# Value products of an attention stage in 64-column halves, gathered by head into two output banks

## The reference

```python
# a: 6 heads of 64; each query sees its keys through three dilated windows, with a bias by distance
# b: 4 heads; p = softmax(s1) - lam * softmax(s2), v has 64 columns, then an rms norm over each head
# c: 6 heads; queries and keys of 64 + 32 columns from low-rank latents, v has 64 columns
attn = concat([a, b, c])        # 512 x 1024
x = layer_norm(alpha * x + attn @ w_o)
x = layer_norm(alpha * x + (silu(x @ w_gate) * (x @ w_up)) @ w_down)
```

## Time and profile before

| | |
|---|---|
| three runs | 1841.17, 1842.97, 1843.08 us |
| the profiled execution | 1841.61 us, span 1839.8 us |
| TensorE busy | 1803.4 us, 98% |
| TensorE weight loads | 1616.9 us, 88% |
| VectorE busy | 1219.3 us, 66% |
| ScalarE busy | 915.2 us, 50% |
| POOL busy | 776.9 us, 42% |
| HBM | 178.10 MB read, 100 GB/s over the span |
| second pair's attention, first layer | 747.3 to 831.1 us |
| second pair's attention, second layer | 1351.1 to 1435.0 us |

### The profile page before, as it was taken

How to read it: one execution, slowest core, us unless ns; L and a number is a source line. 1 busy time by engine, 2 the same in 40 slices (tenths; PEclk the granted TensorE clock), 3 DMA queues, 4 the chain that set the end, 5 groups by cost and what they waited for, 6 DMA issues and landing times.

```text
span 1839.8 us, 32454 instructions
## 1 busy us (share of the span) xinstructions
PE 1803.4 (98%) x12438; PEld 1616.9 (88%) x12438; DVE 1219.3 (66%) x2469; ACT 915.2 (50%) x1789; POOL 776.9 (42%) x601
## 2 busy tenths in 40 slices
PE   9999999999999999999999999999999999999997
PEld 7898888878898888888999998888888899999886
DVE  5797475379364363885999984266379589998533
ACT  4242276474366465873545443327487355454323
POOL 2533262255553354344443335544424344433652
PEclk9999999999999999999999999999999999999999
DMA  8444141123221232102232323222320223323321
GB/s 334 172 172 168 16 115 59 69 74 135 102 48 55 88 133 104 58 2 92 93 109 99 115 92 136 89 88 99 108 87 2 92 70 116 106 102 115 115 92 46
DMA packets 37029, 182.33 MB, mean 99 GB/s; under 512 B 8289, under 2 KB 9185, under 8 KB 18957
## 3 DMA queue, kind: packets, MB, share of 16 engines
q1 hardware_dynamic: 30664, 168.89, 26.6%
q10 hardware_dynamic: 6212, 11.36, 2.0%
HBM read 178.10 MB, written 5.41 MB: 100 GB/s over the span
## 4 chain that ended last, share of the span: by engine, by line
PE 86%; DVE 7%; ACT 4%; issue 2%; POOL 1%; DMA 1%; DVEq 0%; SPq 0%; ACTq 0%
PE ps L1665 17%; PE ps L1667 17%; PE ps L1666 17%; PE ps L2379 7%; PE ps L2381 7%; PE ps L2380 7%; PE ps L2285 3%; PE ps L1745 2%; PE ps L1759 2%; PE ps L2199 2%; PE ps L2303 2%; PE ps L1726 1%; POOL w_lo L874 1%; ACT pt L1131 1%; ACT w_hi L1004 1%
## 5 line engine op out<-in xcount | busy, mean ns | idle before, releaser
L874 POOL TENSOR_TENSOR w_lo<-raw,w_hi 128x512 fp32r<-128x512 f32 (+1 forms) x343 | 477.0, 1423 | 624.2 <-ACT w_hi L1004 624.0
L1004 ACT ACTIVATE w_hi<-raw 128x1024 fp32r<-128x1024 f32 (+3 forms) x174 | 170.9, 1025 | 226.0 <-PE ps L1667 209.1
L980 POOL TENSOR_TENSOR w_lo<-raw,w_hi 128x512 fp32r<-128x512 f32 x80 | 112.7, 1409 | 223.2 <-ACT w_hi L1069 223.0
L1665 PE MATMUL ps<-h_hi,w_lo 128*128 128x512 f32 (+1 forms) x496 | 177.2, 357 | 3.8 <-DVE h_lo L2468 3.7
L1666 PE MATMUL ps<-h_lo,w_hi 128*128 128x512 f32 (+1 forms) x496 | 174.5, 352 | 0.0
L1667 PE MATMUL ps<-h_hi,w_hi 128*128 128x512 f32 (+1 forms) x496 | 174.5, 352 | 0.0
L1665 PE MATMUL ps<-w_hi,hid_lo 128*128 128x512 f32 x352 | 137.1, 390 | 0.0
L1666 PE MATMUL ps<-w_lo,hid_hi 128*128 128x512 f32 x352 | 137.0, 389 | 0.0
L1667 PE MATMUL ps<-w_hi,hid_hi 128*128 128x512 f32 x352 | 136.9, 389 | 0.0
L2468 DVE TENSOR_TENSOR hid_lo<-hid,hid_hi 128x512 fp32r<-128x512 f32 x44 | 65.4, 1530 | 102.1 <-ACT hid_hi L1105 102.1
L1665 PE MATMUL ps<-w_hi,g_lo 128*128 128x512 f32 (+3 forms) x320 | 114.2, 357 | 1.5 <-POOL w_lo L874 1.3
(11 more groups left out here) (375 smaller groups left out, 5548.8 us busy)
## 6 DMA issues: line engine op xcount, KB each, us to landing
raw<-in_tiles SPq DMA_DIRECT2D x139, 1024.0 KB, 4.8
strips<-bias_rows ACTq DMA_DIRECT2D x18, 256.0 KB, 3.6
raw<-in_tiles SPq DMA_DIRECT2D x4, 832.0 KB, 4.1
bias_rows<-bias_row SPq DMA_DIRECT2D x10, 320.0 KB, 10.2
raw<-in_tiles SPq DMA_DIRECT2D x4, 768.0 KB, 5.2
res<-in_x SPq DMA_DIRECT2D x2, 1024.0 KB, 6.5
ln<-in_ln_g ACTq DMA_DIRECT2D x4, 512.0 KB, 3.5
ln<-in_ln_b ACTq DMA_DIRECT2D x4, 512.0 KB, 4.8
```

The costliest lines, as they stand in the source:

```text
L874: pool.tensor_tensor(w_lo[:, i % SPLIT, a:e], raw_of(what)[:, a:e], w_hi[:, i % SPLIT, a:e].bitcast(F32), ALU.subtract).then_inc(s_tile_lo ...
L980: pool.tensor_tensor(lo, quad_of(what[0], j, name), hi.bitcast(F32), ALU.subtract).then_inc(s_pool_piece.sem, s_pool_piece.nth(((what[0], ...
L1004: act.activation(w_hi[:, i % SPLIT, a:b], raw_of(what)[:, a:b], ACT.Copy).then_inc(s_tile_hi.sem, s_tile_hi.nth((what, n)))
L1665: pe.matmul(o, lhs[1], rhs[0], start=first, stop=False)
```

## The change

In the second pair's attention, and there alone:

- The 64 units are put into 13 groups. Group 0 is the first four (head 0 of b, ten products). Each later group ends when four units of a or c are in it, which are one head; units of b that fall between belong to the group as "singles" (12 units, none to two of them in a group). Groups have 10 to 16 products.
- `mix(g)` makes the products of a whole group at once, two ranks after the group's last unit was turned, into one of two output banks (7 for even groups, 5 for odd); each product is two matmuls with 64 columns of weights each, for the two halves of the partitions. The four blocks of the head lie side by side, 65 (group 0: 64) columns each, the singles behind them. One semaphore increment for each group.
- Three banks (2, 1, 3) remain for transpositions and turned chunks; a unit's bank is free when ScalarE has copied it.
- ScalarE's copies need room for a group: they go to two rows of `g_hi`, to `cos2`, behind `vc`, and into the slot of `raw` in which the layer's tile "up" landed. A copy waits for the products of the group two before, or for b of the group of the last b unit of the same i. SP therefore waits for the products of the last group before it loads the tile that takes the slot of "up" (the third tile of the output projection).
- VectorE divides four blocks by one reciprocal of four columns and one multiplication of 128 x 4 x 64 with the reciprocals broadcast; the singles as before. This is done when the group's last unit comes up, three ranks behind.
- The last group's ten products stand behind the first three products of the projection, where the last two units' were.

The core of the diff (left out are the declaration of three semaphores, assertions and the two waits that only change their key):

```diff
-        pt2 = [at(f"pt2_{i}", [P, SEQ], names["g_hi"][0] + 4 * (C_HEADS + i) * SEQ) for i in range(2)]
-        pt2.append(at("pt2_2", [P, SEQ], names["cos2"][0]))
+        pt_rows = at("pt_rows", [P, 2 * SEQ], names["g_hi"][0] + 4 * C_HEADS * SEQ)
+        pt_cos = at("pt_cos", [P, SEQ], names["cos2"][0])
+        pt_vc = at("pt_vc", [P, 384], names["vc"][0] + names["vc"][1])
...
-        N_S, N_T, N_B, N_P = 3, 5, 5, 3
-        S_BANKS, T_BANKS = (4, 6, 0), (2, 1, 3, 5, 7)
+        N_S, N_T, N_B = 3, 3, 5
+        S_BANKS, T_BANKS, OUT_BANKS = (4, 6, 0), (2, 1, 3), (7, 5)
...
+        GROUPS, MIXED, group_of = [[]], {}, {}
+        for r, i in enumerate(RANKS):
+            if len(GROUPS) == 1 and len(GROUPS[0]) == XT or len([q for q in GROUPS[-1] if UNITS[RANKS[q]]["kind"] != "b"]) == XT:
+                GROUPS.append([])
+            GROUPS[-1].append(r)
+            group_of[r] = len(GROUPS) - 1
...
+                if u["kind"] != "b":
+                    a = VW * u["i"]
+                elif g == 0:
+                    a = HD * u["i"]
+                else:
+                    a, singles = VW * XT + HD * singles, singles + 1
+                MIXED[r] = OUT_BANKS[g % 2], a
...
+        def pt_place(y, r):
+
+            u, landing = UNITS[RANKS[r]], raw_of((y, "up"))
+            if u["kind"] == "b":
+                where, a = ((pt_rows, 768), (landing, 1792), (pt_vc, 0), (landing, 1280))[u["i"]]
+            elif group_of[r] % 2 == 0:
+                where, a = landing, (1152, 896, 512, 0)[u["i"]]
+            else:
+                where, a = ((pt_rows, 640), (pt_rows, 384), (pt_rows, 0), (pt_cos, 0))[u["i"]]
+            return where[:, a:a + u["n"]]
+
+        def pt_free(r):
+
+            u = UNITS[RANKS[r]]
+            if u["kind"] == "b":
+                before = [group_of[q] for q in range(r) if UNITS[RANKS[q]]["kind"] == "b" and UNITS[RANKS[q]]["i"] == u["i"]]
+                return before[-1] if before else None
+            return group_of[r] - 2 if group_of[r] > 2 else None
+
+        def copied_by_vector(r):
+            return False
+
+        ended = {what: GROUPS[group_of[r]][-1] for what, r in last_of.items()}
+        out_step = {what: turn_step[r + 3] if r + 3 <= LAST else STEPS for what, r in ended.items()}
...
+                    if before[1] == "up":
+                        sp.wait_ge(s_mixed.sem, s_mixed.at((before[0], len(GROUPS) - 1)))
...
-                        if r >= N_P:
-                            act.wait_ge(s_mixed.sem, s_mixed.at((y, r - N_P)))
-                        act.activation(pt2[r % N_P][:, 0:n], ps[:, TURNED["unit", r], 0:n], ACT.Copy).then_inc(s_pt.sem, s_pt.nth((y, r)))
+                        if not copied_by_vector(r):
+                            act.wait_ge(s_turned.sem, s_turned.at((y, r)))
+                            if pt_free(r) is not None:
+                                act.wait_ge(s_mixed.sem, s_mixed.at((y, pt_free(r))))
+                            act.activation(pt_place(y, r), ps[:, TURNED["unit", r], 0:UNITS[RANKS[r]]["n"]], ACT.Copy).then_inc(s_pt.sem, s_pt.nth((y, r)))
...
-                def mix(r):
...
-                    for j, v in enumerate(u["vs"]):
-                        m = pe.matmul(ps[:, b, 0:v.shape[1]], pt2[r % N_P][:, P * j:P * j + P], v, start=j == 0, stop=j == len(u["vs"]) - 1)
-                    m.then_inc(s_mixed.sem, s_mixed.nth((y, r)))
+                def mix(g):
...
+                    pe.wait_ge(*emptied[OUT_BANKS[g % 2]])
+                    emptied[OUT_BANKS[g % 2]] = s_o_out.after((y, g))
...
+                    for r in GROUPS[g]:
+                        u, (b, a), turned = UNITS[RANKS[r]], MIXED[r], pt_place(y, r)
...
+                            pe.wait_ge(s_pt.sem, s_pt.at((y, r)))
+                        for j, v in enumerate(u["vs"]):
+                            for half in (0, HD):
+                                m = pe.matmul(ps[half:half + HD, b, a:a + v.shape[1]], turned[:, P * j + half:P * j + half + HD], v,
+                                              start=j == 0, stop=j == len(u["vs"]) - 1)
+                    m.then_inc(s_mixed.sem, s_mixed.nth((y, g)))
...
-                        emptied[b] = s_o_out.after((y, r))
+                        emptied[b] = s_pt_b.after((y, r)) if copied_by_vector(r) else s_pt.after((y, r))
...
-                        if r >= 2:
-                            mix(r - 2)
+                        if r - 2 in (group[-1] for group in GROUPS):
+                            mix(group_of[r - 2])
...
-                            if kh == 0 and t == 0 and k < 2:
-                                mix(LAST - 1 + k)
+                            if kh == 0 and t == 0 and k == 0:
+                                mix(len(GROUPS) - 1)
...
                 def rows_out2(r):
 
+                    g = group_of[r]
+                    if r != GROUPS[g][-1]:
+                        return
...
+                    rows = ps[:, b, 0:XT * w].rearrange("p (i d) -> p i d", d=w)
+                    s0 = u["sum"] - u["i"]
+                    totals = recips[:, s0:s0 + XT].unsqueeze(2)
...
+                    dve.wait_ge(s_mixed.sem, s_mixed.at((y, g)))
+                    if g > 0:
+                        step(V.reciprocal(totals, rows[:, :, HD:VW]))
+                    m = V.tensor_tensor(ao[:, :, u["col"]:u["col"] + HD], rows[:, :, 0:HD], totals.broadcast_to((P, XT, HD)), ALU.mult)
+                    for q in singles:
...
+                        m = V.tensor_scalar(ao[:, x["i"], x["col"]:x["col"] + HD], ps[:, b, MIXED[q][1]:MIXED[q][1] + HD],
+                                            recips[:, x["sum"]:x["sum"] + 1], None, ALU.mult)
+                    m.then_inc(s_o_out.sem, s_o_out.nth((y, g)))
```

More of the change, by code:

```diff
@@ L720, in _program @@
             last_of[UNITS[i]["kind"], UNITS[i]["head"]] = r
-        out_step = {what: turn_step[r + 3] if r + 3 <= LAST else STEPS for what, r in last_of.items()}
+        GROUPS, MIXED, group_of = [[]], {}, {}
[4 more added lines that the diff above has]
+            group_of[r] = len(GROUPS) - 1
+        for g, ranks in enumerate(GROUPS):
+            singles = 0
+            for r in ranks:
+                u = UNITS[RANKS[r]]
[6 more added lines that the diff above has]
+                MIXED[r] = OUT_BANKS[g % 2], a
+                assert a + VW <= 512
+            heads = {(UNITS[RANKS[r]]["kind"], UNITS[RANKS[r]]["head"]) for r in ranks if g == 0 or UNITS[RANKS[r]]["kind"] != "b"}
+            assert len(heads) == 1
+        assert all(len(group) >= XT for group in GROUPS) and len(GROUPS) % 2 == 1 and GROUPS[-1][-1] == LAST
+        def pt_place(y, r):
[8 more added lines that the diff above has]
+        def pt_free(r):
+            u = UNITS[RANKS[r]]
+            if u["kind"] == "b":
[6 more added lines that the diff above has]
+        out_step = {what: turn_step[r + 3] if r + 3 <= LAST else STEPS for what, r in ended.items()}
         B_DONE = max(out_step["b", h] for h in range(B_HEADS))
@@ L2269, in turn_chunk @@
                     else:
-                        pe.wait_ge(s_o_out.sem, s_o_out.at((y, max(last_of[w] for w in chunk_heads[k]))))
+                        pe.wait_ge(s_o_out.sem, s_o_out.at((y, max(group_of[last_of[w]] for w in chunk_heads[k]))))
                     for t in range(XT):
@@ L2961, in sub_norm @@
                     if st == B_DONE + 1:
-                        dve.wait_ge(s_o_out.sem, s_o_out.at((y, max(last_of["b", h] for h in range(B_HEADS)))))
+                        dve.wait_ge(s_o_out.sem, s_o_out.at((y, max(group_of[last_of["b", h]] for h in range(B_HEADS)))))
                         step(V.tensor_tensor(sq, o, o, ALU.mult))
@@ L2975, in rows_out2 @@
                 def rows_out2(r):
-                    u = UNITS[RANKS[r]]
-                    total = recips[:, u["sum"]:u["sum"] + 1]
-                    if u["kind"] == "b":
-                        step(V.reciprocal(total, sums[:, u["sum"]:u["sum"] + 1]))
-                    dve.wait_ge(s_mixed.sem, s_mixed.at((y, r)))
-                    if u["kind"] != "b":
-                        step(V.reciprocal(total, ps[:, TURNED["unit", r], HD:VW]))
-                    V.tensor_scalar(ao[:, u["i"], u["col"]:u["col"] + HD], ps[:, TURNED["unit", r], 0:HD], recips[:, u["sum"]:u["sum"] + 1], None,
-                                    ALU.mult).then_inc(s_o_out.sem, s_o_out.nth((y, r)))
+                    g = group_of[r]
@@ new lines, in rows_out2 @@
+                    if r != GROUPS[g][-1]:
+                        return
+                    b = OUT_BANKS[g % 2]
+                    singles = [] if g == 0 else [q for q in GROUPS[g] if UNITS[RANKS[q]]["kind"] == "b"]
+                    u = [UNITS[RANKS[q]] for q in GROUPS[g] if q not in singles][0]
+                    w = HD if g == 0 else VW
+                    rows = ps[:, b, 0:XT * w].rearrange("p (i d) -> p i d", d=w)
+                    s0 = u["sum"] - u["i"]
```

(9 more changed lines are left out.)

22 lines of the change are left out of this document (15 added, 7 removed).

## The result

The changed kernel is **slower**: 1861.37 us, median of four runs (1858.74 to 1863.28), beside 1842.57 for the kernel before on the same chip. The ratio is 1.0102 (95%: 1.0085 to 1.012). The forecast was 1825, with a range that ended at 1837.

What follows compares the result with a forecast made beforehand. TensorE was taken as the bound, busy 80.8 of the stage's 83.8 us; -10.1 - 1.2 + 1.0 + 1.5 = -8.8 us a layer, -17.6 in two, took 1841.61 to 1824.0, plus 1.4 for the median: 1825, range 1817 to 1837.

Steps and rivals of the forecast that it cites:

- turn banks: Transpositions with three banks instead of five wait for VectorE's low part of a turned chunk: 1.5 us a layer, bounds 0 to 5.1.
- TensorE's part: Value products as half records, 31.4 ns each, in 13 runs at 0.16 us for entering and leaving: 10.1 us less a layer.
- VectorE's own work: Scalings and reciprocals in the stage fall from 28.5 to 13.0 us a layer, VectorE's busy time from 70.0 to 54.5.
- VectorE's waits relieved: TensorE's waits for VectorE in front of the transposes shrink: 1.2 us less a layer, bounds 0 and 2.2.
- ScalarE's tie: TensorE at 70.7 us and ScalarE at 65.7 in one ring wait for one another: 1.0 us a layer, bounds 0 to 3.
- The runs starve the others: Rival: ScalarE and VectorE run dry 0.7 us in each of 13 runs, 9 us a layer back, 1842 to 1843; chance 0.06.
- the prediction's own bounds: All unknowns at their best give -12.3 us a layer, 1818.4; at their worst -2.0 a layer, 1839.0.
- The named way to be slower: Rival: half records in the new runs cost as much as full ones, +32 us a layer, near 1907; chance 0.04.
- Waits and queues moved: SP's later loads of the third and fourth output tiles, out-bank waits and the last group's products at the end: cost 0.

Runs made afterwards that it cites:

- e1: The changed kernel with one output bank instead of two and four turn banks instead of three: 1844.76 us, ratio 1.0015 to the kernel before.
- e7: e1 with each group's products in two runs instead of one, 26 runs a layer: 1833.46 us, ratio 0.9957 to the kernel before.
- e14: e7 with the turned units of kind b copied by VectorE instead of ScalarE: 1833.94 us, ratio 0.9956 to the kernel before.
- e13: e7 with the change's own banks, three for turning and two for outputs: 1841.67 us, ratio 0.9998 to the kernel before.
- e17: e7 with whole runs in the last four groups, which have only kind a, 22 runs a layer: 1831.89 us, ratio 0.995 to the kernel before.
- e6: e1 with VectorE's normalisation of a group one rank later: 1850.48 us, ratio 1.0047 to the kernel before.
- e10: e1 with the next step's score in front of each run instead of behind it: 1846.67 us, ratio 1.0025 to the kernel before.
- e11: e7 with the next step's score in front of each run: 1838.27 us, ratio 0.998 to the kernel before.
- e12: e11 with ScalarE's exponential of a step in front of its copy of that step's turned unit: 1839.38 us, ratio 0.9984 to the kernel before.
- e15: The kernel before the change with four probability buffers instead of five, the ring one step shorter: 1863.43 us, ratio 1.0113.
- e3: The changed kernel, still gathered, with each product as one full-width matmul instead of two halves: 1887.57 us, ratio 1.0241 to the kernel before.
- e16: e7 with four probability buffers instead of five, the ring one step shorter: 1848.61 us, ratio 1.0038 to the kernel before.
- e8: e2 with one full-width matmul in place of two halves for each product: 1847.09 us, ratio 1.0028 to the kernel before.
- e2: The changed kernel with each unit's products made alone, in halves, 64 short runs a layer: 1851.71 us, ratio 1.0054 to the kernel before.

## Why the prediction was wrong

The forecast missed by 36.4 us. One more turn bank gives 16.6 of them back (e1); the other 19.8 remain in e1, and there TensorE's waits are 13.7 us a layer where the sum had 4.3, with the turn banks' 1.5 in it. So two terms failed: the turn banks, put at 1.5 us a layer, and the waits for the other engines, where the sum took 1.2 us off for VectorE, added 1.0 for ScalarE, and put nothing for the length of the runs.

The stage in one layer was to fall by 8.8 us, and rose by 9.7: 18.5 us between the two. TensorE's busy time gives 5.7 of them (forecast -10.1, measured -4.4), its waits 12.8 (3.0 + 1.3 forecast, 17.15 measured).

**TensorE's part: right.** Where the clock is up (e1), the busy time of the window falls by 10.7, for 10.9 by the rates of the forecast. Half records at 31 to 33 ns, 13 runs a layer: as said. The price of entering and leaving a run was too low for short runs (about 0.23 for 0.16), which matters little at 13 (0.9 us a layer at most).

**VectorE's own work: right by its records**, 15.4 us less, though its busy time is 58.6 us and not 54.5. **VectorE's waits relieved: wrong in sign.** The forecast took 1.2 us off TensorE's waits on the ground that VectorE has less to do. Waits for the joined pairs went from 1.0 us to 8.2. They are a matter of when VectorE and ScalarE get something to do, not how much: VectorE is busy for 58.6 of 92.5 us and idle in blocks of up to 4.4.

**ScalarE's tie: wrong engine, wrong kind.** It was costed as two engines of nearly equal load. ScalarE is at 69% of the stage, and relieving it in e7, where it is at 82%, changes nothing (e14). The Trainium skill (TensorEngine Tiling (Array Packing), PSUM Bottleneck) says that after such a speed-up the copies out of the banks may become the bound; the trace of the changed kernel doesn't bear that out as a matter of throughput, as neither reader of the banks is above 70%. What it shows instead is a bank held for long: from 770.19, when the chunk is turned, to 775.66.

**Turn banks: the term that was mis-sized.** I wrote 1.5 us out of 0 to 5.1. The wait itself is in those bounds: 5.2 us for low parts after, 2.9 more than with four banks, and 4.0 us of stage in e13. The step that failed is the one worked out from the earlier trace rows, 1.02 us by which the low part would come after the third transposition: it took the lateness of the low part from the kernel before, where VectorE is through with it 4.1 us after the chunk was turned (785.93 to 789.99). After, it is 5.5 us (770.19 to 775.66), ScalarE's high part beginning only 4.1 us after the chunk, and the wait is 2.07. And nothing in the sum had what stands behind it: TensorE's clock falls to 1.2 GHz in that wait (0.61 for 774 to 776, 0.50 from 776 to 780), the run that follows takes nearly double, and the next scores come later. The pair waits don't grow by it (8.2 us for 8.5 in e1); the busy time does, by 6.3 us a layer. There are three such falls: two behind waits for the low part, and one behind a wait of 1.29 us for a pair that e1 has too, at full clock. That the clock was at 1.00 in every window of the kernel before was read as a fact of the kernel; it belonged to its waits, of which none in the stage is over 0.61 us.

**The runs starve the others: the nearest rival, and the other failed step.** It had the place (a run with no score and no transposition in it) and a price of 9 us a layer, and was given 0.06, because three score banks spoke against it. By e1 against e7 the price is 7.9 us of waits a layer for one run instead of two, less the cost of more runs: 5.2 us a layer with the 28 records put on the same side, 11.3 us of time in the two layers. With that alone the kernel comes out near no change, as e1 does (1844.76, 0.15% slower) and as the rival said (1842 to 1843). Slower by 1% comes from the runs and the turn banks together, each making the other dearer: 8.3 us a layer for the bank with long runs, 4.1 with short ones, where the clock stays at 1.00. The rivals were priced one at a time. The range ended at 1837, below the 1839.0 that the prediction's own bounds give, and the result lies outside both.

**The named way to be slower** (halves that don't overlap) is excluded: records stand 31 to 33 ns apart wherever the clock is 1.00.

**Waits and queues moved: right.** In the 30 us behind the stage no engine waits for a tile's landing. Outside the two windows 2.3 us are new in all, 1.8 of them the ten last products for three.

**What stays open.** Shown is that the pair waits grow with the length of a run (0.3 us for 64 runs a layer, 3.6 for 26, 8.5 for 13), that long runs cost nothing measurable in the part without pairs (e17), and that the waits don't go away with another place of the normalisation in VectorE's queue (e6), one score earlier (e10, e11), another order on ScalarE (e12) or less load on it (e14). By what path a run makes a pair late stays open. My reading, argued and not shown, is that a run of 2 us is longer than what the four steps between a pair's scores and its transposition hold in reserve. Cutting one of those steps brings the pair waits of e7 from 3.6 to 8.6 us and those of the kernel before from 1.0 to 4.3; but all waits grow alike in both, and the loss that this reading forecast for e7 didn't come. A ring of one step more would test it; it needs another buffer for probabilities, and wasn't tried.

## What to carry to other kernels

When work is gathered to make it cheaper, price the longest stretch in which the other engines get nothing new against what the ring between them holds, and price each bank taken away by the latest reader of the kernel after, not of the one before. Then add what a wait can do to TensorE's clock: a stage at 1.00 with waits up to 0.6 us held stretches at 1.2 GHz once waits of 1.3 to 2 us were in it, and these cost more (6.3 us a layer) than the waits that the missing bank added (3.4). Between the two extremes there was a better length here: half a group where the others depend on it, a whole one where they don't.

## What had not been expected of the hardware

TensorE's granted clock fell to its lower level inside a stage in which it was busy for four fifths of the time. It was there in the run at 777.89 behind a wait of 2.07 us, and in the one at 788.60 behind a wait of only 1.29 us (44 records in 2.59 us, 59 ns each), but not behind the one of 1.28 us before the run at 760.29. In e1 eight waits of 1.04 to 1.63 us in the same stage passed with the clock at 1.00, and in e15 one of 1.50 us brought it to 0.50 for over 12 us. Longer waits passed as well, one after and one in e3, both with the clock at 1.00 in the wait and in the 3 us behind it, and both again in the second layer:

```profile
830.67 0.41 PE L2364 MATMUL ps<-ident,sc 128*128 128x128 f32 x2 [1.82 <-ACT sc L1565]
```

```profile
806.00 0.63 PE L2362 MATMUL ps<-ident,sc 128*128 128x128 f32 x4 [2.02 <-DVE g_lo L2527]
```

Nor do the two layers of one execution always agree: in e16 a wait of 1.75 us is followed by the lower level in the first layer (772.07) and not in the second (1380.32), and e11 falls behind one of 1.07 us (807.49) in the first layer alone. Every fall in the stages read stands behind a wait of 1.07 us or more; above that the length of the wait doesn't decide, and what does, these traces don't tell.

Entering and leaving a run of half records costs about 0.23 us when it has 4 to 16 records (e8 against e2), more than the 0.16 read off a run of 36.
